# Two transformer blocks on one core: earlier table arithmetic, and five groups of transposes moved from TensorE to VectorE

## The chip, the core and the metric

The kernel runs on one core of one Trainium2 chip. Everything is float32. The metric is the device time of one launch in microseconds: the median of three runs is 2400.58 us (2400.37 to 2401.02).

## The reference

A sequence of 256 tokens, 2048 wide, goes through a gated delta-rule block with a Fourier branch and an MLP, and then through a second block with spatial gating, a state-space branch and cross attention. All weights together are 396 MB. Cut to what the change touches:

```python
# first block
qkv = silu(centred_short_conv(concat([q, k, v]), conv_w))       # 5 taps along the tokens, per channel
q = l2_norm(heads(q)) * DN_HEAD_DIM ** -0.5; k = l2_norm(heads(k)); v = heads(v)
x = x + (gate_a * y_a + gate_f * y_f) @ w_o[l]                   # y is "y_rows" before it is turned
# second block
dt = exp(log_dt); lam_bar = exp(lam * dt)                        # "tables" of the state-space branch
b_bar = ((lam_bar - 1) / lam)[:, :, None] * b_mat
k = (rms_norm_2(mem, mem_g) @ w_k).reshape(b, n_mem, XA_HEADS, XA_HEAD_DIM)   # "km"
v = (rms_norm_2(mem, mem_g) @ w_v).reshape(...)                               # "vm"
scores = einsum('bshd,bmhd->bhsm', qh, k) * XA_HEAD_DIM ** -0.5
merged = sum(gates * branch, axis=2); out = merged @ w_out
```

## The kernel before

The weights are cut into 396 units of 1 MB (128 partitions x 2048 numbers, four blocks of 128 rows by 512 columns). TensorE works through them in one fixed order. A product in float32 is made of three in TensorE's fast 32-bit format: the weight is split into `w_hi` and the rest `w_lo`, the activation likewise (`a_hi`, `a_lo` or `b_hi`, `b_lo` or `m_hi`, `m_lo`), and a unit is 24 matmuls of 128x512 (lines 2161, 2164, 2167): three products, four blocks, two halves of the 256 tokens.

Four engines share a unit n. SyncE issues the load of unit n into one of the buffers `raw` once TensorE is through with unit n - 4 (`weight`, L620 to L624, a wait on `pe_used`). ScalarE rounds it to `w_hi` (L794), VectorE forms `w_lo` in place of `raw` (L1253). Both do so two units ahead of TensorE: the split of unit n + 2 stands in slot n of their programs. TensorE waits on VectorE's `w_lo` (`lo_split`, L2143) at the start of a unit.

All other work is cut into steps, and `schedule()` gives each step a place, 2n (in the middle of unit n on TensorE, ahead of the split on the two other engines) or 2n + 1 (at the end of unit n, behind the split). Each engine runs its own part of a step at that place, in order; nothing is reordered at run time. A wait inside a step therefore holds up everything that stands behind it on that engine. This is true of SyncE too: a load of spilled rows that waits (`load_vm` for the attention's values, L699) has the next weights behind it.

The steps that the change touches:

- `conv_in`, `conv_silu`, `conv_norm`, `conv_root`: q and k of one half (512 columns, four heads) are turned to channels by tokens, by eight transposes on TensorE (L2272) which ScalarE copies into the padded tile `padT` (L955). VectorE applies the five taps (L1556, L1559), ScalarE the silu and the squares (L964, L970), TensorE sums the squares in 16 matmuls of one column (L2280). Half 0 of q and k lies at units 12 and 16, half 1 at units 48 and 52. v goes the same way and is not changed.
- `y_in(0)` and `merge_in(0)`: the first quarter (512 columns) of `y_rows`, the operand of `w_o` (units 88 to 103) and `w_out` (units 380 to 395). TensorE turns it in eight transposes (L2178), ScalarE writes `b_hi` (L808), VectorE `b_lo` (L1268).
- `ssm_small(0)` and `(1)`: the state-space branch's tables, 12 and 28 small VectorE operations on 128x32 numbers (L1734 to L1812) and a few on ScalarE, at slots 242 and 244.
- `xa_k`: the attention's keys `km_rows` are turned to `kmT` by 16 transposes on TensorE (L2398) and four copies on ScalarE (L1049) at the end of unit 333. The first to read them are the scores (`xa_score`, L2457) ahead of unit 338. `vm` is loaded over the place of `km_rows`, so `load_vm` waits until the keys are turned.

VectorE has its own transpose of 32x32 blocks: `turn_strips` (L1293) turns 512 columns of 256 rows in 16 instructions of 32 partitions x 256 numbers each.

Of the kernel before, what the change touches and what calls it, by code (L numbers as in the profile page):

```python
# [163 lines left out]
def schedule():  # L164
# [38 lines left out]
    for n in range(4):  # L203
# [4 lines left out]
        put_at(2 * end("w_dn_up", n) + 2, "y_in", n)  # L208
# [48 lines left out]
    put(end("xa_wv", 1) + 2, "ssm_small", 0)  # L257
    put(end("xa_wv", 1) + 4, "ssm_small", 1)
# [90 lines left out]
def build(nc, t_in, out, old, new):  # L349

    with ExitStack() as ctx:
# [432 lines left out]
        def _(act):  # L784
# [287 lines left out]
            def glu_rest():  # L1072
# [40 lines left out]
        def _(pool):  # L1113
# [1493 lines left out]
```

## Time and profile before

| | before |
|---|---|
| median of 3 runs | 2400.58 us (2400.37 to 2401.02) |
| the profiled execution's own time | 2403.19 us |
| its span in the trace | 2401.0 us |
| TensorE busy | 2379.5 us, 99% |
| VectorE busy | 1744.6 us, 73% |
| ScalarE busy | 1031.4 us, 43% |
| GpSimd busy | 272.6 us, 11% |
| share of the last chain: PE, DVE, DMA | 95%, 3%, 1% |
| moved by DMA | 475.16 MB, mean 198 GB/s |

The span is what the trace covers; the profiled execution took 2.19 us more than its span. Of the chain that ended last 95% is TensorE's own work, so nearly every microsecond of TensorE's work or idle time is one of the kernel's. The time of a wait has to be looked for at single units, since the shares are averages over 396 of them.

### The profile page before, as it was taken

What the parts mean: (1) busy time and instruction counts of PE and PEld (TensorE: products, weight loads), DVE (VectorE), ACT (ScalarE), POOL (GpSimd) and SP (SyncE); (2) the same over time, 40 slices, a digit from 0 to 9 for tenths busy, and PEclk for the clock granted to TensorE, in tenths of its full rate; (3) what the DMA queues carried; (4) which work ended last, traced back from release to release, by engine and by line L of the source; (5) the groups of instructions that cost most, each with busy time, mean ns of one, the idle gap of its engine ahead of it and who ended that gap; (6) DMA issues with size and microseconds to landing.
All of it is one profiled execution on the core that took longest, in us unless ns stands there. A gap on an engine that the chain in (4) does not pass through costs nothing.

```text
span 2401.0 us, 29968 instructions
## 1 busy us (share of the span) xinstructions
PE 2379.5 (99%) x12578; PEld 1950.2 (81%) x12578; DVE 1744.6 (73%) x1990; ACT 1031.4 (43%) x857; POOL 272.6 (11%) x226
## 2 busy tenths in 40 slices
PE   8999999999999999999999999999999999999998
PEld 7888788878888888888888888777777788888886
DVE  6465557557697887786766788989999967458865
ACT  5553345334344544444444435443334444544432
POOL 1002201210000000000000000055556400000000
PEclk9999999999999999999999999999999999999999
DMA  7343354347655555555555556565555586566753
GB/s 268 131 167 133 141 184 167 117 156 258 258 193 189 195 194 211 193 193 193 193 193 193 193 211 218 198 237 185 196 193 197 181 298 244 184 232 234 257 196 140
DMA packets 84230, 475.16 MB, mean 198 GB/s; under 512 B 8704, under 2 KB 8832, under 8 KB 32512
## 3 DMA queue, kind: packets, MB, share of 16 engines
q1 hardware_dynamic: 84096, 473.25, 55.5%
q8 instruction: 99, 1.62, 0.3%
q14 instruction: 35, 0.29, 0.0%
HBM read 450.15 MB, written 23.07 MB: 197 GB/s over the span
## 4 chain that ended last, share of the span: by engine, by line
PE 95%; DVE 3%; DMA 1%; issue 0%; ACT 0%; DVEq 0%; SPq 0%; ACTq 0%
PE acc L2161 29%; PE acc L2167 29%; PE acc L2164 29%; PE banks L2306 2%; PE banks L2355 1%; DVE w_lo L1253 1%; PE banks L2422 1%; PE banks L2435 1%; DMA raw<-in_w 1%; PE banks L2178 1%; DMA spilled<-stage 1%; PE banks L2475 0%; PE banks L2457 0%; PE banks L2280 0%; DMA gate_in<-spilled 0%
## 5 line engine op out<-in xcount | busy, mean ns | idle before, releaser
L1253 DVE TENSOR_TENSOR w_lo<-raw,w_hi 128x2048 fp32r<-128x2048 f32 x394 | 908.7, 2308 | 395.3 <-ACT w_hi L794 392.6
L794 ACT ACTIVATE w_hi<-raw 128x2048 fp32r<-128x2048 f32 x394 | 752.8, 1915 | 656.0 <-DMA raw<-in_w 655.8
L2161 PE MATMUL acc<-w_hi,a_hi 128*128 128x512 f32 x2112 | 838.2, 397 | 2.7 <-ACT a_hi L814 1.6
L2164 PE MATMUL acc<-w_lo,a_hi 128*128 128x512 f32 x2112 | 823.8, 390 | 0.0
L2167 PE MATMUL acc<-w_hi,a_lo 128*128 128x512 f32 x2112 | 823.7, 390 | 0.0
L2161 PEld LDWEIGHTS acc<-w_hi,a_hi 128*128 128x128 f32 x2112 | 397.0, 188 | 100.4 <-issue 15.4
L2167 PEld LDWEIGHTS acc<-w_hi,a_lo 128*128 128x128 f32 x2112 | 396.8, 188 | 84.7 <-DVE a_lo L1289 0.3
L2164 PEld LDWEIGHTS acc<-w_lo,a_hi 128*128 128x128 f32 x2112 | 397.4, 188 | 79.1
L2161 PE MATMUL acc<-w_hi,b_hi 128*128 128x512 f32 x928 | 361.7, 390 | 0.0
L2167 PE MATMUL acc<-w_hi,b_lo 128*128 128x512 f32 x928 | 361.1, 389 | 0.0
L2164 PE MATMUL acc<-w_lo,b_hi 128*128 128x512 f32 x928 | 361.0, 389 | 0.0
L2167 PEld LDWEIGHTS acc<-w_hi,b_lo 128*128 128x128 f32 x928 | 174.2, 188 | 36.1
L2164 PEld LDWEIGHTS acc<-w_lo,b_hi 128*128 128x128 f32 x928 | 174.2, 188 | 36.1
L2161 PEld LDWEIGHTS acc<-w_hi,b_hi 128*128 128x128 f32 x928 | 174.2, 188 | 36.0
L1300 DVE STREAM_TRANSPOSE b_raw<-hidden 32x256 f32<-32x256 f32 x256 | 111.5, 436 | 7.5
L1234 POOL MEMSET c_out<- 128x2048 f32 x1 | 1.8, 1817 | 1006.7 <-DMA spilled<-stage_b 1006.7
L893 ACT ACTIVATE stage<-acc,stats 128x512 f32<-128x512 f32 x72 | 45.6, 686 | 130.2 <-PE acc L2167 130.2
L1483 DVE TENSOR_TENSOR x_rows<-x_rows,acc 128x512 f32<-128x512 f32 x72 | 46.2, 683 | 31.1 <-PE acc L2167 31.0
L1204 POOL TENSOR_TENSOR rot<-pow_a,pow_b 128x256 f32<-128x256 f32 x32 | 47.6, 1488 | 176.8 <-DVE s_out L1918 130.4
L1904 DVE TENSOR_TENSOR_SCAN prod<-rad,prod 128x256 f32<-128x256 f32 x64 | 57.4, 956 | 0.6
L2161 PE MATMUL acc<-w_hi,m_hi 128*128 128x512 f32 x128 | 51.4, 401 | 2.2 <-DVE w_lo L1253 2.2
L1300 DVE STREAM_TRANSPOSE a_raw<-x_rows 32x256 f32<-32x256 f32 x112 | 48.8, 436 | 3.3
(353 smaller groups left out, 1681.3 us busy)
## 6 DMA issues: line engine op xcount, KB each, us to landing
raw<-in_w SPq DMA_DIRECT2D x395, 1024.0 KB, 4.8
spilled<-stage SPq DMA_DIRECT2D x72, 256.0 KB, 5.9
gate_in<-spilled SPq DMA_DIRECT2D x20, 512.0 KB, 5.8
x_rows<-in_x SPq DMA_DIRECT2D x4, 512.0 KB, 8.4
x_rows<-in_x SPq DMA_DIRECT2D x1, 2048.0 KB, 9.4
mem_rows<-in_mem SPq DMA_DIRECT2D x2, 1024.0 KB, 5.8
spilled<-stage_b SPq DMA_DIRECT2D x8, 256.0 KB, 5.9
out<-y_rows SPq DMA_DIRECT2D x3, 512.0 KB, 2.7
```

The source lines that it names most:

```text
L794: act.activation(w_hi[:, n % HIGH, :], raw[:, n % RAW, :], ACT.Copy)\
L893: act.activation(dst, src, func, scale=rms(norm, t)).then_inc(act_emptied, 1)
L1204: pool.tensor_tensor(c_[:, g], pa[0][:, g], pb[0][:, g], ALU.mult).then_inc(pool_done, me.done())
L1253: dve.tensor_tensor(w_lo[:, n % RAW, :], raw[:, n % RAW, :], w_hi[:, n % HIGH, :].bitcast(F32), ALU.subtract).then_inc(lo_split, 1)
L1300: dve.transpose(dst, src).then_inc(dve_done, me.done(*done_as))
L1483: ins = dve.tensor_tensor(x_rows[:, t, cs], x_rows[:, t, cs], src, ALU.add)
L1904: dve.tensor_tensor_scan(pr[z + 1][:, g], r_, pr[z][:, g], 0.0, ALU.mult, ALU.add)\
L2161: pe.matmul(o, hi[:, tk], wh, start=first, stop=False)
L2164: pe.matmul(o, hi[:, tk], wl, start=False, stop=False)
L2167: ins = pe.matmul(o, lo[:, tk], wh, start=False, stop=last)
L2178: ins = pe.transpose(b[:, q * P:(q + 1) * P], src(q), ident)
L2306: ins = pe.matmul(b[rs, cs], lhs[rs, cs], rhs(k, rs), start=True, stop=True)
```

## The change

Four kinds of work are moved. (1) `ssm_small(0)` and `(1)` run at slots 234 and 237 instead of 242 and 244. (2) q and k are turned by VectorE, straight from `qkv` into `padT`, by a new step `conv_turn`; the steps behind it (`conv_in`, `conv_silu`, `conv_norm`, `conv_root`) are given places three to five later. (3) The first quarters of y and of merge are turned by VectorE (`turn_first`, `first_hi`, `first_lo`). (4) The keys are turned by VectorE (`turn_plain("km", ...)`), and `load_vm` and the scores wait for VectorE.

```diff
     for half in (0, 1):
         for x, name in enumerate(("w_q", "w_k")):
             at = 2 * end(name, half) + 1
-            put_at(at, "conv_in", half, x, 0)
-            put_at(at + 2, "conv_in", half, x, 1)
-            put_at(at + 4, "conv_silu", half, x)
-            put_at(at + 6, "conv_norm", half, x)
+            for part in range(4):
+                put_at(at + part, "conv_turn", half, x, part)
+            put_at(at + 4, "conv_in", half, x, 0)
+            put_at(at + 5, "conv_in", half, x, 1)
+            put_at(at + 7, "conv_silu", half, x)
+            put_at(at + 9, "conv_norm", half, x)
             if x:
-                put_at(at + 8, "conv_root", half)
+                put_at(at + 11, "conv_root", half)
...
-        put_at(2 * end("w_dn_up", n) + 2, "y_in", n)
+        if n:
+            put_at(2 * end("w_dn_up", n) + 2, "y_in", n)
...
-        put_at(2 * end("w_branch1", n) + 2, "merge_in", n)
+        if n:
+            put_at(2 * end("w_branch1", n) + 2, "merge_in", n)
     f = end("w_dn_up", 3)
     put(f + 1, "load_mem", 0)
+    for tag, name in (("y", "w_dn_up"), ("merge", "w_branch1")):
+        at = 2 * end(name, 0) + 2
+        for part in range(6):
+            put_at(at + part, "turn_first", tag, part)
+        put_at(at + 6, "first_hi", tag)
+        put_at(at + 8, "first_lo", tag)
...
-    put(end("xa_wv", 1) + 2, "ssm_small", 0)
-    put(end("xa_wv", 1) + 4, "ssm_small", 1)
+    put(end("xa_wv", 0) - 2, "ssm_small", 0)
+    put(end("xa_wv", 0) + 1, "ssm_small", 1)
...
     for part in range(8):
         put_at(2 * a + 17 + part, "turn_plain", "sg", part)
+        put_at(2 * a + 25 + part, "turn_plain", "km", part)
     put_at(2 * a + 26, "plain_hi", "sg")
     put_at(2 * a + 28, "plain_lo", "sg")
     put(a + 10, "gelu_turn")
     a = max(a + 13, end("w2_xg", 1) + 1)
     put(a - 1, "load_xq")
-    put(a, "xa_k")
     put(a + 1, "load_vm")
...
             def load_mem(t):
                 if t == 0:
                     sp.wait_ge(pe_done, me.at("y.T"))
...
             def load_vm():
-                sp.wait_ge(pe_done, me.at("km.T"))
+                sp.wait_ge(dve_done, me.at("km.T"))
                 load_rows(vm, "xa_wv", loaded["vm"])
...
+            def first_hi(tag):
+                act.wait_ge(dve_done, me.at(f"{tag}.first.T"))
+                for t in range(NT):
+                    at = (slice(None), slice(0, 4), slice(t * P, (t + 1) * P))
+                    act.activation(b_hi[0][at], b_raw[0][at], ACT.Copy).then_inc(act_done, me.done(f"{tag}.{t}.hi"))
...
+            def conv_turn(half, x, part):
+                if part == 0:
+                    dve.wait_ge(act_emptied, emptied(INDEX[(("w_q", "w_k")[x], half)], "act"))
+                    dve.wait_ge(pool_done, me.at("pad1" if half else "pad0"))
+                    if x == 0 and half:
+                        dve.wait_ge(pe_done, me.at("scan0.3.out.PE"))
+                    if x:
+                        dve.wait_ge(dve_done, me.at(f"conv{half}0.sum"))
+                rows = padT[:, :, 2:2 + T]
+                turn_strips(qkv[:, x], rows, 4 * part, 4, (f"conv{half}{x}.turned",))
+
             def conv_in(half, x, part):
-                dve.wait_ge(act_done, me.at(f"conv{half}{x}.pad0", f"conv{half}{x}.pad1"))
+                if x < 2:
...
+            def turn_first(tag, part):
+                name = {"y": "w_fourier", "merge": "w_branch0"}[tag]
+                if part == 0:
+                    dve.wait_ge(pe_used, end(name, 3))
+                    dve.wait_ge(dve_done, me.at("w_dn_up0.y" if tag == "y" else "w_branch10.y"))
+                turn_strips(y_rows[:, :, 0:NW], b_raw[0][:, 0:4, :], 3 * part, min(3, 16 - 3 * part), (f"{tag}.first.T",))
+
+            def first_lo(tag):
+                for t in range(NT):
+                    at = (slice(None), slice(0, 4), slice(t * P, (t + 1) * P))
+                    dve.wait_ge(act_done, me.at(f"{tag}.{t}.hi"))
+                    dve.tensor_tensor(b_lo[0][at], b_raw[0][at], b_hi[0][at].bitcast(F32), ALU.subtract)\
+                        .then_inc(dve_done, me.done(f"{tag}.{t}.lo"))
...
             def turn_plain(tag, part):
                 raw_rows = PLAIN[tag][0]
                 if part == 0:
                     if tag == "xo":
                         dve.wait_ge(pe_used, end("w2_gate2", 3))
-                    dve.wait_ge(dve_done, me.at({"sg": "sg.gated", "xo": "xo.rows", "glu": "glu.rows"}[tag]))
+                    if tag == "km":
+                        dve.wait_ge(loaded["km"], 32)
+                        dve.wait_ge(dve_done, me.at("sg.T"))
+                    else:
+                        dve.wait_ge(dve_done, me.at({"sg": "sg.gated", "xo": "xo.rows", "glu": "glu.rows"}[tag]))
```

Before, VectorE's program in half 1 of the convolution reads, from the six splits that end with unit 46's on (`w_lo`; `convT<-padT` are the taps, `nrm` the norms):

```order
L1253 TENSOR_TENSOR w_lo<-raw,w_hi 128x2048 x6
L1556 TENSOR_SCALAR convT<-padT,small 128x256 x2
L1559 SCALAR_TENSOR_TENSOR convT<-padT,small,convT 128x256 x8
L1253 TENSOR_TENSOR w_lo<-raw,w_hi 128x2048
L1556 TENSOR_SCALAR convT<-padT,small 128x256 x2
L1559 SCALAR_TENSOR_TENSOR convT<-padT,small,convT 128x256 x8
L1253 TENSOR_TENSOR w_lo<-raw,w_hi 128x2048 x2
L1568 TENSOR_SCALAR nrm<-banks 128x2x4
L1576 RECIPROCAL nrm<-nrm 128x2x4
L1253 TENSOR_TENSOR w_lo<-raw,w_hi 128x2048
```

Now the turns (`padT<-qkv`, eight instructions for half of the 512 columns) stand ahead of the splits, and the two sets of taps come together:

```order
L1271 TENSOR_TENSOR w_lo<-raw,w_hi 128x2048 x6
L1318 STREAM_TRANSPOSE padT<-qkv 32x2x4x32 x8
L1271 TENSOR_TENSOR w_lo<-raw,w_hi 128x2048
L1318 STREAM_TRANSPOSE padT<-qkv 32x2x4x32 x8
L1271 TENSOR_TENSOR w_lo<-raw,w_hi 128x2048
L1588 TENSOR_SCALAR convT<-padT,small 128x256 x2
L1591 SCALAR_TENSOR_TENSOR convT<-padT,small,convT 128x256 x8
L1588 TENSOR_SCALAR convT<-padT,small 128x256 x2
L1591 SCALAR_TENSOR_TENSOR convT<-padT,small,convT 128x256 x8
L1271 TENSOR_TENSOR w_lo<-raw,w_hi 128x2048 x2
L1318 STREAM_TRANSPOSE padT<-qkv 32x2x4x32 x4
L1600 TENSOR_SCALAR nrm<-banks 128x2x4
```

Between the splits of units 46 and 47 there was one set of taps and there are now eight turns; both sets of taps stand behind unit 48's split. The first sum of squares (`nrm<-banks`) moves behind the turns of k.

At the state-space tables VectorE's program read, ahead of the splits of units 238, 239 and 240 (`a_raw<-x_rows` are turns of the next block's input, `a_lo` its low part):

```order
L1300 STREAM_TRANSPOSE a_raw<-x_rows 32x2x4x32 x2
L1322 TENSOR_TENSOR a_raw<-a_raw,stats 128x4x128 x2
L1300 STREAM_TRANSPOSE a_raw<-x_rows 32x2x4x32 x2
L1253 TENSOR_TENSOR w_lo<-raw,w_hi 128x2048
L1300 STREAM_TRANSPOSE a_raw<-x_rows 32x2x4x32 x4
L1253 TENSOR_TENSOR w_lo<-raw,w_hi 128x2048
L1329 TENSOR_TENSOR a_lo<-a_raw,a_hi 128x4x128 x2
L1300 STREAM_TRANSPOSE a_raw<-x_rows 32x2x4x32 x4
L1253 TENSOR_TENSOR w_lo<-raw,w_hi 128x2048
```

Now the 28 operations of `ssm_small(1)` (`ssm_t`) follow the split of unit 239, the first six of them shown, and unit 240's split comes behind all of them:

```order
L1271 TENSOR_TENSOR w_lo<-raw,w_hi 128x2048
L1318 STREAM_TRANSPOSE a_raw<-x_rows 32x2x4x32 x4
L1271 TENSOR_TENSOR w_lo<-raw,w_hi 128x2048
L1347 TENSOR_TENSOR a_lo<-a_raw,a_hi 128x4x128 x2
L1318 STREAM_TRANSPOSE a_raw<-x_rows 32x2x4x32 x2
L1788 TENSOR_TENSOR ssm_t<-ssm_t 128x32
L1790 TENSOR_SCALAR ssm_t<-ssm_t 128x32
L1792 TENSOR_SCALAR ssm_t<-ssm_t 128x32
L1794 TENSOR_SCALAR ssm_t<-ssm_t 128x32
L1796 TENSOR_TENSOR ssm_t<-ssm_t 128x32
L1798 TENSOR_TENSOR ssm_t<-ssm_t 128x32
```

The 12 operations of `ssm_small(0)` stand in the same way between the splits of units 236 and 237. Both groups came behind the split of unit 243 before.

At the attention's keys VectorE's program had, from the split of unit 333 on (`b_raw<-av` are turns of the spatial gate, `b_lo<-b_raw` their low part):

```order
L1253 TENSOR_TENSOR w_lo<-raw,w_hi 128x2048
L2013 STREAM_TRANSPOSE b_raw<-av 32x2x8x32 x4
L1253 TENSOR_TENSOR w_lo<-raw,w_hi 128x2048 x2
L2020 TENSOR_TENSOR b_lo<-b_raw,b_hi 128x4x128 x4
L1253 TENSOR_TENSOR w_lo<-raw,w_hi 128x2048 x4
L1979 TENSOR_REDUCE stats<-banks 128x2
```

Now it has four groups of turned keys (`kmT<-km_rows`, 16 instructions in all) between the splits of units 334 to 338:

```order
L1271 TENSOR_TENSOR w_lo<-raw,w_hi 128x2048
L2063 STREAM_TRANSPOSE b_raw<-av 32x2x8x32 x4
L1271 TENSOR_TENSOR w_lo<-raw,w_hi 128x2048
L2063 STREAM_TRANSPOSE kmT<-km_rows 32x2x8x32 x4
L1271 TENSOR_TENSOR w_lo<-raw,w_hi 128x2048
L2063 STREAM_TRANSPOSE kmT<-km_rows 32x2x8x32 x4
L2070 TENSOR_TENSOR b_lo<-b_raw,b_hi 128x4x128 x4
L1271 TENSOR_TENSOR w_lo<-raw,w_hi 128x2048
L2063 STREAM_TRANSPOSE kmT<-km_rows 32x2x8x32 x4
L1271 TENSOR_TENSOR w_lo<-raw,w_hi 128x2048
L2063 STREAM_TRANSPOSE kmT<-km_rows 32x2x8x32 x4
L1271 TENSOR_TENSOR w_lo<-raw,w_hi 128x2048 x2
```

The last turned keys stand behind the split of unit 337 in VectorE's program. On SyncE the order does not move, but the semaphore that `vm` waits for does. Before:

```order
L624 DMA raw<-in_w 128x2048 [waits pe_used] x2
L634 DMA vm<-spilled 128x2x512 [waits spill_stored1,spill_stored0,pe_done]
L634 DMA vm<-spilled 128x2x512 [waits spill_stored3,spill_stored2]
L624 DMA raw<-in_w 128x2048 [waits pe_used] x2
L741 DMA spilled<-stage 128x512 [waits act_emptied] x2
L624 DMA raw<-in_w 128x2048 [waits pe_used] x4
```

Now (the two weights behind `vm` are units 338 and 339):

```order
L635 DMA raw<-in_w 128x2048 [waits pe_used] x2
L645 DMA vm<-spilled 128x2x512 [waits spill_stored1,spill_stored0,dve_done]
L645 DMA vm<-spilled 128x2x512 [waits spill_stored3,spill_stored2]
L635 DMA raw<-in_w 128x2048 [waits pe_used] x2
L753 DMA spilled<-stage 128x512 [waits act_emptied] x2
L635 DMA raw<-in_w 128x2048 [waits pe_used] x4
```

`pe_done` has become `dve_done` in the row of `vm`, and the rows behind it are the same.

## Rows read from the trace of the kernel before

**Rows 1.** The page, busy time of each engine and weight issues to landing.

```profile
PE 2379.5 (99%) x12578; PEld 1950.2 (81%) x12578; DVE 1744.6 (73%) x1990; ACT 1031.4 (43%) x857; POOL 272.6 (11%) x226
...
raw<-in_w SPq DMA_DIRECT2D x395, 1024.0 KB, 4.8
```

**Rows 2.** Chain of waits: start, duration, what, xcount.

```profile
121.99 1.68 PE banks L2280 x16
...
361.36 0.87 PE banks L2272 x8
...
2027.61 1.75 PE banks L2398 x16
```

**Rows 3.** Timeline of PE: start, duration, instruction, idle time before it.

```profile
1462.99 0.39 PE L2161 MATMUL acc<-w_hi,m_hi 128*128 128x512 f32 x1
...
1501.80 0.40 PE L2167 MATMUL acc<-w_hi,m_lo 128*128 128x512 f32 x1
...
1504.36 0.80 PE L2161 MATMUL acc<-w_hi,m_hi 128*128 128x512 f32 x1 [2.17 <-DVE w_lo L1253]
...
1511.57 0.39 PE L2161 MATMUL acc<-w_hi,a_hi 128*128 128x512 f32 x1
...
1527.66 0.39 PE L2167 MATMUL acc<-w_hi,a_lo 128*128 128x512 f32 x1
...
1529.17 0.47 PE L2161 MATMUL acc<-w_hi,a_hi 128*128 128x512 f32 x1 [1.12 <-DVE pow_b L1845]
```

**Rows 4.** Windows, all engines; PEclk is the granted clock, 1.00 full.

```profile
1500.00:1520.00 20.00, 17.83 (x72) 14.23 (x71) 17.57 (x29) 8.28 (x7) 0.77 (x1) 0.91 0.54 188
```

**Rows 5.** Timeline of DVE between 1436 and 1505.

```profile
1436.04 2.29 DVE L1253 TENSOR_TENSOR w_lo<-raw,w_hi 128x2048 fp32r<-128x2048 f32 x1 [1.14 <-ACT w_hi L794]
...
1455.22 2.29 DVE L1253 TENSOR_TENSOR w_lo<-raw,w_hi 128x2048 fp32r<-128x2048 f32 x1
...
1466.29 2.29 DVE L1253 TENSOR_TENSOR w_lo<-raw,w_hi 128x2048 fp32r<-128x2048 f32 x1 [1.50 <-ACT w_hi L794]
...
1481.12 0.18 DVE L1734 TENSOR_SCALAR ssm_t<-small 128x32 f32<-128x32 f32 x1
...
1495.53 0.20 DVE L1756 TENSOR_TENSOR ssm_t<-ssm_t 128x32 f32<-128x32 f32 x1
...
1502.02 2.28 DVE L1253 TENSOR_TENSOR w_lo<-raw,w_hi 128x2048 fp32r<-128x2048 f32 x1
```

**Rows 6.** Timeline of DVE around the convolution and two other places.

```profile
334.62 2.29 DVE L1253 TENSOR_TENSOR w_lo<-raw,w_hi 128x2048 fp32r<-128x2048 f32 x1 [4.92 <-ACT w_hi L794]
...
387.42 0.61 DVE L1556 TENSOR_SCALAR convT<-padT,small 128x256 f32<-128x256 f32 x2 [2.33 <-ACT padT L955]
...
394.81 2.28 DVE L1253 TENSOR_TENSOR w_lo<-raw,w_hi 128x2048 fp32r<-128x2048 f32 x1
...
1398.00 1.83 DVE L1300 STREAM_TRANSPOSE a_raw<-x_rows 32x256 f32<-32x256 f32 x4
...
619.07 1.29 DVE L1268 TENSOR_TENSOR b_lo<-banks,b_hi 128x512 fp32r<-128x512 f32 x2 [2.52 <-ACT b_hi L808]
```

**Rows 7.** Timeline of ACT between 372 and 374.

```profile
372.68 1.06 ACT L964 ACTIVATE kT<-convT 128x1024 f32<-128x1024 f32 x1 [4.10 <-DVE convT L1559]
```

**Rows 8.** Timeline of PE at units 53 and 88.

```profile
386.45 0.48 PE L2161 MATMUL acc<-w_hi,a_hi 128*128 128x512 f32 x1
...
633.20 0.39 PE L2161 MATMUL acc<-w_hi,b_hi 128*128 128x512 f32 x1
```

**Rows 9.** Timeline of DVE where the attention's keys are due.

```profile
2018.99 2.92 DVE L2013 STREAM_TRANSPOSE b_raw<-av 32x512 f32<-32x512 f32 x4
```

**Rows 10.** Timeline of SP: two weight issues behind a load of rows.

```profile
2175.21 4.86 SPq L624 DMA_DIRECT2D raw<-in_w  x2
```

**Rows 11.** Timeline of ACT: the split that waited for the first.

```profile
2182.51 1.92 ACT L794 ACTIVATE w_hi<-raw 128x2048 fp32r<-128x2048 f32 x1 [8.67 <-DMA raw<-in_w]
```

**Rows 12.** Timeline of PE at unit 338.

```profile
2054.30 0.58 PE L2161 MATMUL acc<-w_hi,a_hi 128*128 128x512 f32 x1
```

More of the change, by code:

```diff
@@ L574, in build @@
                  "xo": (a_raw[:, 0:KW, :], a_hi[:, 0:KW, :], a_lo[:, 0:KW, :]),
+                 "km": (kmT[:, :, :],),
                  "glu": (a_raw[:, KW:, :], a_hi[:, KW:, :], a_lo[:, KW:, :])}
@@ L665, in load_mem @@
                     sp.wait_ge(pe_done, me.at("y.T"))
+                    sp.wait_ge(dve_done, me.at("y.first.T"))
                 else:
@@ L949, in conv_in @@
             def conv_in(half, x, part):
+                if x < 2:
+                    return
                 for b in range(2 if part == 0 else 0):
@@ L1043, in turned @@
             def turned(tag, dst, scale):
-                if tag == "km":
-                    act.wait_ge(dve_done, me.at("sg.T"))
                 for j in range(4):
@@ L1090, in _ @@
                      "sg_norm": lambda part: root("sgn", 64, NT) if part == 0 else None,
-                     "gelu_turn": gelu_turn, "plain_hi": plain_hi,
-                     "xa_k": lambda: turned("km", kmT, 1.0), "xa_q": lambda: turned("xq", xqT, 1.0 / 16),
+                     "gelu_turn": gelu_turn, "plain_hi": plain_hi, "first_hi": first_hi,
+                     "xa_q": lambda: turned("xq", xqT, 1.0 / 16),
                      "xa_score": xa_score, "xa_prob": xa_prob, "xa_out": xa_out,
@@ L1234, in ssm_small @@
                 pool.memset(c_out[:, :, :, :], 0.0).then_inc(pool_done, me.done("c_out.zero"))
-            steps = {"conv_in": lambda half, x, part: pads(half) if (x, part) == (0, 0) else None,
+            steps = {"conv_turn": lambda half, x, part: pads(half) if (x, part) == (0, 0) else None,
                      "key_rows": key_rows, "gram": gram, "decay": decay, "turn": turn, "solve_x": solve_x, "fold": fold,
@@ L1539, in fourier @@
                         .then_inc(dve_done, me.done(f"fourier{g}.lo"))
+            def conv_turn(half, x, part):
[8 more added lines that the diff above has]
+                turn_strips(qkv[:, x], rows, 4 * part, 4, (f"conv{half}{x}.turned",))
             def conv_in(half, x, part):
-                dve.wait_ge(act_done, me.at(f"conv{half}{x}.pad0", f"conv{half}{x}.pad1"))
+                if x < 2:
+                    dve.wait_ge(dve_done, me.at(f"conv{half}{x}.turned"))
+                else:
+                    dve.wait_ge(act_done, me.at(f"conv{half}{x}.pad0", f"conv{half}{x}.pad1"))
                 dve.wait_ge(pool_done, me.at("pad1" if half else "pad0"))
@@ L2042, in tables @@
                     .then_inc(dve_done, me.done("w_sc.lo"))
-            steps = {"tables": tables, "scalars": scalars, "fourier": fourier, "conv_in": conv_in,
+            steps = {"tables": tables, "scalars": scalars, "fourier": fourier, "conv_turn": conv_turn, "conv_in": conv_in,
                      "conv_norm": conv_norm, "conv_root": conv_root, "key_rows": key_rows, "decay": decay, "turn": turn, "solve_x": solve_x,
@@ L2059, in _ @@
                      "ssm_small": ssm_small, "ssm": ssm, "sg_norm": sg_norm, "sg_mix": sg_mix,
-                     "gelu_turn": gelu_turn, "xa_score": xa_score, "turn_plain": turn_plain, "plain_lo": plain_lo,
+                     "gelu_turn": gelu_turn, "xa_score": xa_score, "turn_plain": turn_plain, "turn_first": turn_first, "first_lo": first_lo, "plain_lo": plain_lo,
                      "xa_gate": xa_gate, "glu_rest": glu_rest, "glu_gate": glu_gate}
@@ L2263, in conv_in @@
             def conv_in(half, x, part):
-                if part:
+                if part or x < 2:
                     return
@@ L2452, in xa_score @@
             def xa_score(h):
-                pe.wait_ge(act_done, me.at("km.3.t", "xq.3.t"))
+                pe.wait_ge(dve_done, me.at("km.T"))
+                pe.wait_ge(act_done, me.at("xq.3.t"))
                 b = take_bank("xs", h, f"xa{h}.exp")
@@ L2485, in glu_rest @@
                     ins.then_inc(pe_done, me.done(f"gr.{j}.T", "gelu_rows.T"))
-            def xa_k():
-                pe.wait_ge(loaded["km"], 32)
-                turned("km", lambda t, k: km_rows[:, t, k * P:(k + 1) * P])
             def xa_q():
@@ L2500, in _ @@
                      "ssm_u": ssm_u, "ssm": ssm, "sg_mix": sg_mix,
-                     "xa_k": xa_k, "xa_q": xa_q, "xa_score": xa_score, "xa_prob": xa_prob,
+                     "xa_q": xa_q, "xa_score": xa_score, "xa_prob": xa_prob,
                      "xa_out": xa_out, "glu_rest": glu_rest,
```

3 lines of the change are left out of this document (2 added, 1 removed).

## The prediction

> **What bounds the kernel now.** I read the page first: TensorE is busy for 99% of the span [rows 1]. The chain of waits comes next: its small pieces are the transposes and column sums that stand between units, 0.87 us for eight transposes, 1.75 for sixteen, 1.68 for sixteen column sums [rows 2]. They are on the path, and so is what they become if VectorE is late: the timeline of PE shows the two places near the tables where it waited (2.17 and 1.12 us) [rows 3]. So each part is a balance: TensorE work removed, against how late VectorE's split `w_lo` comes at the next units. For the second I rebuild VectorE's queue from its timeline in the new order and compare it with the start of the unit on PE.
>
> **Removed from TensorE.** Eight transposes go at each of four places of the convolution (3.48 us) and at the two first quarters (1.74), sixteen at the keys (1.75) [rows 2]. Total 6.97 us. The column sums only move one and a half units later.
>
> **Tables.** Before, unit 247 started 2.56 us after the last matmul of unit 246, where 0.23 is usual: 2.33 lost. It then took 7.21 us (1504.36 to 1511.57) [rows 3]. Usual is 5.58: from 1462.99 to 1501.80 are seven units less one matmul, 167 steps of 0.2324, and 24 of these. The difference, 1.63, is the clock: PE was granted 0.91 of full speed in the window from 1500 to 1520, which means that it ran at 1.2 GHz for part of it, after the 2.17 us without work [rows 4, 3]. The second wait cost 1.51 − 0.23 = 1.28 [rows 3], and the clock did not fall after it. Together 5.24 us come back if the operations no longer hold anything up there. I count on all of it, because 9 us less stand ahead of units 247 to 251 on VectorE; if only the second wait stays, 1.28 less comes back.
>
> In their new place 28 operations (1495.53 to 1502.02, 6.49 us, 0.232 each) and 12 more (2.7 at the same step) stand ahead of the split of unit 240 [rows 5]. That split began at 1455.22, with no idle time before it; the next idle time of VectorE in the row behind is 1.50 at 1466.29. So all 9.2 us push it: it starts at 1464.4 and ends 2.3 later, at 1466.7. PE wants it at 1462.99 [rows 3]. A wait of 3.7 us is new. It is longer than the 2.17 after which the clock fell, so I add the same 1.63. This part is then −5.24 + 3.7 + 1.63 = +0.1, or −1.5 if the clock stays up. ScalarE's share costs nothing: its table loads lie beside VectorE's queue, which is the later one; were that cover gone they would add to the same wait. From 1466.29 on VectorE has idle time to catch up, and unit 241 follows in time.
>
> **Convolution.** Turning 512 columns takes 16 instructions. Four of the same shape took 1.83, so eight take 3.7 and sixteen 7.4 [rows 6]. Two sets of taps take 394.81 − 387.42 = 7.4 [rows 6]. In half 1 VectorE starts the split of unit 46 at 334.62 [rows 6]. In the new order: +2.3 split, +3.7 turns, +2.3 split (unit 47), +3.7 turns, +2.2 split (48), +7.4 taps, so q's taps end at 356.3. Then the silu, 1.06, squares of the same size, and the split of 1.92 on ScalarE follow [rows 7, 11], 4.1 in all, and the split of unit 50 can start at 360.4. Behind it: 2.3 + 1.9 + 0.4 (norm) + 1.9 + 2.3 + 3.7 + 2.2 + 7.4 = 22.1, and the split of unit 53 ends at 384.85. PE wants it at 386.45 [rows 8] less two groups of transposes (1.74) and less the 1.70 of column sums that now come behind unit 53: 383.0. New wait 1.8. The same reckoning gives 0.1 at unit 49, and in half 0 0.25 at unit 21 and 0.5 at unit 23. Together 2.65 against 3.48 removed: −0.8. Its bounds: −3.5 if VectorE is never late, and +0.8 plus 1.6 if the clock falls at unit 53.
>
> **First quarters.** The turns wait for `y_rows`, and VectorE's queue sets the end. The second quarter's `b_lo` starts at 619.07 [rows 6] and ends at 620.3; three turns (1.4), unit 87's split (2.3), two products and a sum of the gates (2.5), and the last turn follow: 626.9. ScalarE's `first_hi` ends at 627.9 and its split at 629.8, VectorE's split of unit 88 at 632.1, a pair `b_lo` and the pair `first_lo` (pairs like these took 1.29 [rows 6], started 1.25 apart) at 634.6. PE wants the operand at 633.20 [rows 8]. The transposes taken away here lay at unit 83, ahead of all of this, so both sides come 0.87 earlier and the difference stays. New wait 1.4. Merge has the same steps in the same order. Two times 1.4 against 1.74 removed: +1.06. Bounds: −1.74 if the operand is in time, +2.9 with 2.3 each.
>
> **Keys.** VectorE turns them in 16 instructions, four in 2.92 [rows 9]. After the four at 2018.99 its queue has no gap in the new order: unit 334's split (2021.93 to 2024.26), then 2.94 turns, 2.33 split, 2.94, 2.45 low part, 2.33, 2.94, 2.33, 2.94: the keys are turned at 2045.5. TensorE had done so by 2029.4 [rows 2]. The scores come later and do not wait. But the load of `vm` waits for the keys on SyncE, and behind it stand the weights of units 338 and 339, as the two rows of the change show. They are issued at 2046.5, some 12 us later than before. What a weight takes then: the row of the page says 4.8 us, with nothing ahead of it [rows 1]. Two weights issued at 2175.21 right behind a 1 MB load of rows, as here, let ScalarE start at 2182.51, 7.3 later [rows 10, 11]. I take 7.3, the case that is like this one: split on ScalarE from 2053.8 to 2055.75, on VectorE until 2058.05. PE wants unit 338 at 2054.30 [rows 12] − 1.75 = 2052.55. New wait 5.5 us, 3.0 with a landing in 4.8, and 1.63 for the clock, as after 2.17 us. Net: −1.75 counted above, +7.1 here.
>
> The Trainium skill ("DMA: Bandwidth & Descriptors", Queues, rings and completion order) says that the descriptors of an issuing engine's row are consumed in ring order on each DMA engine. By that rule the weight's data start behind those of `vm`, which speaks for 7.3 and not 4.8; the rows at 2175 agree.
>
> **Sum.** −6.97 −5.24 + (3.7 + 1.63) + 2.65 + 2.8 + (5.5 + 1.63) = +5.7 us. The profiled execution took 2403.19 and would take 2408.9; the median lies 2.6 lower, so I predict 2400.58 + 5.7 = **2406.3 us**. What a measurement here can tell from no change I take as 0.2%, 4.8 us.
>
> **Rivals.**
> - *Cheaper waits.* The weights behind `vm` land in 4.8 us (−2.5) and the clock stays up after both long waits (−3.3): 2400.5. For it: the 4.8 of the page is the median of 395 [rows 1], and the clock did not fall after 1.12 us [rows 3]. Against it: it fell after 2.17, and both new waits are longer than that.
> - *The change does what it looks like and VectorE is never late* (the other side). All that is removed comes back, 6.97 + 5.24 = 12.2: 2388.4. It needs VectorE's idle time, 27% of the span, to lie at these places. It decides at unit 240 and at unit 338: below 5.5 us of pushed work ahead of unit 240's split, and with the keys turned before 2040, no wait arises. Against it: VectorE's rows have no gap where the 9.2 us and the 11.8 us of key turns are put.
> - *The clock falls at the shorter waits too.* Units 53, 88 and 380 wait for 1.4 to 1.8 us, between the 1.12 that did not lower the clock and the 2.17 that did [rows 3]. At 1.63 each, 4.9 more: 2411.2, and with the operands another 0.85 late at both quarters 2412.9. Against it: 1.12 did nothing.
> - *Transposes count as rest.* Eight transposes of v end right ahead of unit 53's wait, so that TensorE does no large matmul for 0.87 + 1.8 = 2.7 us there, more than the 2.17 that lowered the clock [rows 2, 3]. Then the clock falls there alone: 2406.3 + 1.6 = 2407.9.
>
> The Trainium skill ("TensorE: Matmul & The Clock Gate", Part 4: PE-mode transpose) says that transposes do not count as TensorE being busy. That is the mechanism of the last rival; the trace shows eight transposes at 0.109 us each [rows 2] and no wait behind such a group, so it decides nothing.
>
> **How the numbers follow.** Forecast 0.48, its own range 2403.5 to 2409.5, from landing and clock each going one way. The bound of 4.8 us lies at 2405.4, inside it, so two thirds of it are slower (0.32) and a third is within (0.16). Cheaper waits 0.20, within. The change does what it looks like 0.09, faster. Lower clock at short waits 0.13 and transposes as rest 0.06, slower. Remaining 0.04: small mistakes in the queues that cancel, within. Faster 0.09, same 0.40, slower 0.51. The range from 2400 to 2411.5 leaves out the 0.09 and the upper part of the rival with the lower clock, and holds the bounds of landing and clock.
>
> **What the new profile would show.** PE: no wait left at unit 247, one of about 3.7 at unit 240 released by `w_lo`, one of 3 to 5.5 at unit 338 with a granted clock under 1.00 in the window behind each. SP: `vm` issued at about 2045 in the old times, with two weights right behind. Waits of 1 to 2 us at units 53, 88 and 380. The prediction is wrong if unit 338 starts without a wait, which would mean that the keys were turned by 2040 or that the weights do not stand behind `vm`, or if unit 240 waits for less than 1 us.

## The result and the profile after

The changed kernel takes 2412.35 us (2410.87 to 2413.80, 5 runs) against 2400.58 before (2400.32 to 2401.52, 5 runs): a ratio of 1.0045, 95% interval 1.0033 to 1.0056. It is slower, by more than the 4.8 us that can be told from no change. The forecast was 2406.3, with a range up to 2411.5: the direction was right, the amount about half of what came, and the median lies 0.85 above the range. In a second set of runs the same kernel took 2411.56 (2410.10 to 2412.68) beside 2401.44 before, where one of the 21 runs of before took 3411.25 us and leaves the median where it is.

The profiled execution took 2411.5, with a span of 2409.7, 8.7 more than before's. The page, where TensorE has 64 matmul instructions less and 5.3 us less work than in [rows 1]:

```profile
PE 2374.2 (99%) x12514; PEld 1942.2 (81%) x12514; DVE 1799.2 (75%) x2102; ACT 1025.9 (43%) x845; POOL 267.9 (11%) x226
```

The timeline of PE shows what came in their place. The columns are those of [rows 3]; these are all the places after the first 60 us where TensorE waited for more than 1 us:

```profile
383.88 0.50 PE L2211 MATMUL acc<-w_hi,a_hi 128*128 128x512 f32 x1 [1.44 <-DVE w_lo L1271]
```

```profile
633.04 0.47 PE L2211 MATMUL acc<-w_hi,b_hi 128*128 128x512 f32 x1 [1.48 <-issue]
```

```profile
1462.70 0.40 PE L2217 MATMUL acc<-w_hi,m_lo 128*128 128x512 f32 x1
...
1466.99 0.77 PE L2211 MATMUL acc<-w_hi,m_hi 128*128 128x512 f32 x1 [3.89 <-DVE w_lo L1271]
...
1467.55 0.63 PE L2214 MATMUL acc<-w_lo,m_hi 128*128 128x512 f32 x1
...
1474.04 0.40 PE L2211 MATMUL acc<-w_hi,m_hi 128*128 128x512 f32 x1
```

```profile
1531.10 0.47 PE L2211 MATMUL acc<-w_hi,a_hi 128*128 128x512 f32 x1 [1.55 <-DVE pow_b L1877]
```

```profile
2060.68 0.79 PE L2211 MATMUL acc<-w_hi,a_hi 128*128 128x512 f32 x1 [5.08 <-DVE w_lo L1271]
...
2061.28 0.63 PE L2214 MATMUL acc<-w_lo,a_hi 128*128 128x512 f32 x1
...
2068.17 0.47 PE L2211 MATMUL acc<-w_hi,a_hi 128*128 128x512 f32 x1
```

```profile
2310.47 0.47 PE L2211 MATMUL acc<-w_hi,b_hi 128*128 128x512 f32 x1 [1.48 <-issue]
```

In order of time these are units 53 (1.44 us idle), 88 (1.48), 240 (3.89), 251 (1.55), 338 (5.08) and 380 (1.48). Unit 247, which had waited 2.17 [rows 3], is gone from the list; unit 251 is still on it, but not for the same reason (see the experiments). The second matmul of units 240 and 338 takes 0.63 instead of 0.39, which is the lower clock of 1.2 GHz, and the granted clock of these stretches is 0.91, as it was behind unit 247 before [rows 4]. Behind the four waits of 1.4 to 1.6 us no matmul is slow. At units 88 and 380 the profile names no releaser ("issue"). VectorE's own timeline has it: the low part of the first quarter (`first_lo`, L2040) ends at 632.93, 0.11 before unit 88 starts.

```profile
631.65 1.28 DVE L2040 TENSOR_TENSOR b_lo<-b_raw,b_hi 128x512 fp32r<-128x512 f32 x2
```

The windows:

```profile
1460.00:1480.00 20.00, 16.11 (x64) 12.71 (x63) 18.93 (x36) 6.90 (x7) 0.00 (x0) 0.91 0.49 165
...
2050.00:2070.00 20.00, 14.92 (x62) 11.95 (x61) 7.83 (x7) 9.48 (x10) 0.00 (x0) 0.91 0.79 290
```

How VectorE got late at unit 240, in its own timeline (unit 239's split, the turn ahead of the 28 operations, the turn behind them, unit 240's split; [rows 5] had that split at 1455.22):

```profile
1452.49 2.29 DVE L1271 TENSOR_TENSOR w_lo<-raw,w_hi 128x2048 fp32r<-128x2048 f32 x1
...
1456.02 0.90 DVE L1318 STREAM_TRANSPOSE a_raw<-x_rows 32x256 f32<-32x256 f32 x2
...
1463.61 0.90 DVE L1318 STREAM_TRANSPOSE a_raw<-x_rows 32x256 f32<-32x256 f32 x2
...
1464.55 2.29 DVE L1271 TENSOR_TENSOR w_lo<-raw,w_hi 128x2048 fp32r<-128x2048 f32 x1
```

Nothing is idle between them, and the split ends at 1466.84, 0.15 before TensorE starts.

And at the keys. VectorE's last turn, SyncE's load of `vm` with the two weights behind it, and ScalarE's first split of these:

```profile
2045.33 2.92 DVE L2063 STREAM_TRANSPOSE kmT<-km_rows 32x512 f32<-32x512 f32 x4
```

```profile
2048.28 0.89 SPq L645 DMA_DIRECT2D vm<-spilled  x2
...
2049.22 0.93 SPq L635 DMA_DIRECT2D raw<-in_w  x2
```

```profile
2056.40 1.91 ACT L806 ACTIVATE w_hi<-raw 128x2048 fp32r<-128x2048 f32 x1 [11.92 <-DMA raw<-in_w]
```

From the issue of the weights at 2049.22 to the split are 7.2 us, about the 7.3 behind the 1 MB load at 2175 [rows 10, 11], and ScalarE had been idle for 11.92 us.

### The profile page after: what moved, and what is told of

Same layout as the page of the kernel before. It is cut to its first block, busy times and chain, and to the rows that moved or that the text cites. A ratio compares the mean times of both kernels' runs of the same rounds, so it can differ in the third digit from the quotient of the medians.

```text
span 2409.7 us, 29932 instructions
## 1 busy us (share of the span) xinstructions
PE 2374.2 (99%) x12514; PEld 1942.2 (81%) x12514; DVE 1799.2 (75%) x2102; ACT 1025.9 (43%) x845; POOL 267.9 (11%) x226
## 4 chain that ended last, share of the span: by engine, by line
PE 87%; DVE 8%; DMA 2%; issue 1%; ACT 1%; SPq 0%; DVEq 0%; ACTq 0%
PE acc L2211 27%; PE acc L2214 26%; PE acc L2217 26%; DVE w_lo L1271 2%; PE banks L2356 2%; DMA raw<-in_w 2%; PE banks L2405 1%; DVE convT L1591 1%; DVE padT L1318 1%; ACT w_hi L806 1%; PE banks L2472 1%; PE banks L2485 1%; DVE a_raw L1318 1%; DVE kmT L2063 0%; PE banks L2228 0%
## 5 line engine op out<-in xcount | busy, mean ns | idle before, releaser
L2211 PE MATMUL acc<-w_hi,a_hi 128*128 128x512 f32 x2112 | 838.7, 397 | 11.8 <-DVE w_lo L1271 8.4
```

Of the source, the lines that this page charges most:

```text
L2211: pe.matmul(o, hi[:, tk], wh, start=first, stop=False)
```

## The experiments

All times of one table line were taken beside the kernel before on the same chip. The first set (the four kernels with one part undone) had 18 runs of before (median 2401.58), the second (changed again, vm later, tables at 240) 21 (2401.44), the third (the last three) 27 (2401.89). The changed kernel was not run in the first set, so what a part is worth when undone is a difference between two sets. The changed kernel lay 11.8 us above before beside the result and 10.1 in the second set: differences of one or two microseconds are therefore read from the traces, and the medians only say whether they agree.

| kernel | median us (lowest to highest), runs | ratio to before, 95% |
|---|---|---|
| changed, again | 2411.56 (2410.10 to 2412.68), 5 | 1.0042 [1.0030, 1.0055] |
| changed, keys on TensorE | 2406.95 (2404.39 to 2408.22), 11 | 1.0022 [1.0013, 1.0030] |
| changed, tables at the old slots | 2407.99 (2406.74 to 2408.95), 8 | 1.0026 [1.0016, 1.0036] |
| changed, first quarters on TensorE | 2409.95 (2408.32 to 2410.22), 5 | 1.0033 [1.0021, 1.0046] |
| changed, convolution on TensorE | 2410.08 (2409.65 to 2413.69), 5 | 1.0035 [1.0022, 1.0049] |
| changed, vm loaded later | 2405.21 (2403.05 to 2407.62), 11 | 1.0016 [1.0007, 1.0026] |
| changed, tables at 240, c_in earlier | 2406.83 (2402.94 to 2408.95), 11 | 1.0022 [1.0013, 1.0031] |
| all mended | 2396.81 (2394.92 to 2397.66), 11 | 0.9978 [0.9969, 0.9987] |
| before with the mended tables alone | 2397.36 (2397.00 to 2399.57), 11 | 0.9985 [0.9976, 0.9994] |
| all mended, convolution on TensorE | 2396.44 (2395.00 to 2397.64), 11 | 0.9978 [0.9970, 0.9987] |

To read the traces beside each other I take TensorE's starts of units as marks and the time from one mark to the next. It is free of the first 60 us: the start of unit 8, at 57 to 58.5 us, varied by 1.5 us among the thirteen traces. The times, in us:

| stretch (from unit to unit) | before, twice | changed, twice | what it holds |
|---|---|---|---|
| 10 to 14 | 32.53, 32.49 | 30.01, 30.01 | transposes of q, half 0 |
| 15 to 60 | 327.63, 327.64 | 328.09, 328.19 | rest of the convolution |
| 82 to 92 | 58.00, 58.00 | 58.84, 58.85 | first quarter of y |
| 235 to 251 | 94.06, 92.86 | 96.06, 96.31 | tables |
| 333 to 342 | 58.69, 58.69 | 63.78, 63.45 | keys |
| 374 to 384 | 58.00, 58.00 | 58.87, 58.86 | first quarter of merge |

**Undoing one part at a time.** The four kernels are the changed one with one part of the diff taken back.

Keys on TensorE:

```diff
-        put_at(2 * a + 25 + part, "turn_plain", "km", part)
+    put(a, "xa_k")
...
-                sp.wait_ge(dve_done, me.at("km.T"))
+                sp.wait_ge(pe_done, me.at("km.T"))
```

> The changed kernel with one part undone: the keys are turned by TensorE again and vm waits for TensorE. Theory (the load of vm holds up two weights, unit 338 waits 5.2 us and the clock falls behind it): the waits of 5.2 and 1.5 us go and 1.75 us of transposes come back, 5.0 us faster than the changed kernel, 2407.4; no step longer than 0.3 us is left between units 334 and 340. Rival (the keys on VectorE are a gain and the loss is made elsewhere): 1.75 us slower, 2414.1.

It came out 4.6 us below the changed kernel (2406.95 against 2411.56), against 5.0 expected, and the stretch from 333 to 342 is 58.70 again, as before the change. The rival is out.

Tables at the old slots:

```diff
-    put(end("xa_wv", 0) - 2, "ssm_small", 0)
-    put(end("xa_wv", 0) + 1, "ssm_small", 1)
+    put(end("xa_wv", 1) + 2, "ssm_small", 0)
+    put(end("xa_wv", 1) + 4, "ssm_small", 1)
```

> The changed kernel with the table operations at their old slots 242 and 244. Theory (in their new place they make a wait of 4.1 at unit 240 and a slow unit 240 of 1.5, in the old one 2.3 and 1.6 at unit 247, and the wait at unit 251 has another cause but is 0.4 shorter): 2.0 us faster, 2410.3. Rival of the prediction (both old waits come back, 5.24, against 5.3): no difference, 2412.3.

3.6 us below the changed kernel, more than the 2.0. Neither sentence had it: unit 247 waited again, but for 1.11 us and not for 2.17, and the clock stayed at 1.00. The stretch from 235 to 251 took 92.40, which is 3.7 and 3.9 less than in the two traces of the changed kernel.

```profile
1502.54 0.50 PE L2211 MATMUL acc<-w_hi,m_hi 128*128 128x512 f32 x1 [1.11 <-DVE w_lo L1271]
```

```profile
1500.00:1520.00 20.00, 18.73 (x81) 14.76 (x80) 17.71 (x24) 8.29 (x7) 1.82 (x1) 1.00 0.60 211
```

First quarters on TensorE (`y_in` and `merge_in` at n = 0 again, `turn_first`, `first_hi` and `first_lo` not scheduled):

```diff
-        if n:
-            put_at(2 * end("w_dn_up", n) + 2, "y_in", n)
+        put_at(2 * end("w_dn_up", n) + 2, "y_in", n)
```

> The changed kernel with both first quarters turned by TensorE again. Theory (a wait of 1.65 at units 88 and 380 against 0.9 of transposes each): 1.5 us faster, 2410.8. Rival (in most runs the clock falls at both waits too, though not in the profiled one): 1.5 + 3.3 = 4.8 us faster, 2407.6, and a higher mean granted clock than the changed kernel has. Other rival (VectorE hides it): 1.7 slower, 2414.1.

1.6 us below the changed kernel. That alone would be within the spread of the sets; the traces show it, since both stretches are 58.00 again, 0.84 and 0.87 less. No slow matmul stood behind units 88 and 380 in the seven traces that wait there, so the rival with the lower clock is not borne out.

Convolution on TensorE (`conv_turn` not scheduled, `conv_in`, `conv_silu`, `conv_norm`, `conv_root` at their old places, the copies into `padT` on ScalarE again):

```diff
-            for part in range(4):
-                put_at(at + part, "conv_turn", half, x, part)
-            put_at(at + 4, "conv_in", half, x, 0)
+            put_at(at, "conv_in", half, x, 0)
```

> The changed kernel with q and k of the convolution turned by TensorE again. Theory (3.5 us of transposes against waits of 0.6, 0.5, 0.1 and 1.5 us at units 21, 23, 49 and 53, all at full clock): 0.9 us slower, 2413.2. Rival (the clock falls behind the wait of unit 53 in most runs): 0.7 us faster, 2411.6. Where the clock falls near 100 us for the transposes of q, 1.6 slower again, as in the profiled run of before: 2414.8.

The median is 1.5 us below the changed kernel, where 0.9 above was expected, on 5 runs that spread over 4.0. By the marks the part is worth -0.4 to the changed kernel: from 10 to 14 30.86 here against 30.01, and from 15 to 60 327.6 against 328.1. What varies is the clock near 100 us. Before's two traces lost 1.65 there (32.5 against 30.86), this one nothing:

```profile
90.00:110.00 20.00, 20.00 (x122) 17.70 (x122) 11.22 (x21) 10.73 (x15) 0.00 (x0) 1.00 0.40 138
```

while the kernel with the quarters undone, which has no transposes of q at all there, lost 1.6:

```profile
90.00:110.00 20.00, 20.00 (x107) 17.50 (x106) 11.01 (x18) 8.70 (x10) 0.00 (x0) 0.91 0.38 145
```

So the low clock there does not belong to the transposes. In before's first trace it shows ahead of them too: the four matmuls of 128x130 that end the stretch of small ones took 1.07 us at 98.66 and 0.61 at 88.85. The clock fell in 3 of 8 traces with q on VectorE and in 3 of 5 with q on TensorE.

**The kernel before, in a second trace**, since undoing the tables had given a wait of another length.

> The kernel before once more, one look. Theory (the wait of 2.3 at unit 247 hangs on when unit 244's weight lands, and the profile of before caught a late one): here that weight is split on ScalarE up to 1.8 us earlier against unit 244, the wait is 1.3, and the clock does not fall behind it: about 2400.5, 2.6 below the profiled time. Rival (the wait and the fall are fixed costs, and before's profile is slow for another reason): the wait of 2.3 and the slow unit 247 are there again.

It took 2401.56, and the wait at unit 247 was 1.56 us and not 2.17. The clock did not fall. The next wait, at unit 251, was longer than in [rows 3]:

```profile
1503.51 0.51 PE L2161 MATMUL acc<-w_hi,m_hi 128*128 128x512 f32 x1 [1.56 <-DVE w_lo L1253]
...
1527.72 0.47 PE L2161 MATMUL acc<-w_hi,a_hi 128*128 128x512 f32 x1 [1.65 <-DVE pow_b L1845]
```

```profile
1500.00:1520.00 20.00, 18.29 (x79) 14.44 (x78) 17.60 (x27) 8.28 (x7) 1.81 (x1) 1.00 0.64 217
```

The cause of the difference stands 27 us ahead of the wait's end. Unit 244's split on VectorE waited for ScalarE 0.83 us here; in before's profile it waited longer and started 0.85 later, and there is no idle time on VectorE between it and unit 247. Of the 0.85, 0.25 is TensorE's own shift (1501.55 against 1501.80), and 0.6 is the difference of the waits:

```profile
1476.94 2.29 DVE L1253 TENSOR_TENSOR w_lo<-raw,w_hi 128x2048 fp32r<-128x2048 f32 x1 [0.83 <-ACT w_hi L794]
```

```profile
1477.79 2.29 DVE L1253 TENSOR_TENSOR w_lo<-raw,w_hi 128x2048 fp32r<-128x2048 f32 x1 [1.27 <-ACT w_hi L794]
```

ScalarE in turn had waited for the weight (4.27 here, 4.72 there). It was issued at 1468.51 here and at 1468.75 there, and ScalarE started 6.5 and 7.1 us later. Of the 2.33 us in the first profile some 0.6 were thus a later weight's. The slow clock came with them, in this one trace only; that the length of the wait brought it is the likely reading, but no run tests it. The theory named the right place and missed the size (1.7 and not 1.3).

**The changed kernel again.**

> The changed kernel once more, beside the runs that the next ones are compared with. If the single steps of the traces are all there is, its profile shows the same waits (1.5 at unit 53, 1.65 at 88 and 380, 4.1 at 240, 1.7 at 251, 5.2 at 338) and the slow clock behind 240 and 338 alone. If the 3 us by which its median stands above the step count come from the clock, its slow stretches are longer than 1.5 us each or more in number.

The same six waits stood there, with slow matmuls behind units 240 and 338 alone. But in the other kernels of this study the slow clock did not always cost 1.5 us. In six traces the start of unit 241 came 7.05, 7.22, 8.20, 7.23, 8.32 and 8.45 us after that of unit 240 (5.57 at full clock), and in six that of 339 came 7.49, 7.58, 7.54, 8.63, 8.38 and 8.31 after 338 (6.03). Means: 2.2 and 2.0 lost, and not 1.63. The long one, from the trace of the kernel with `vm` later, in which the granted clock of the window was lower:

```profile
1460.00:1480.00 20.00, 16.11 (x58) 12.59 (x57) 19.12 (x32) 6.78 (x7) 0.00 (x0) 0.83 0.38 140
```

**The load of vm behind the two weights.** The keys stay on VectorE.

```diff
-    put(a + 1, "load_vm")
+    put(a + 3, "load_vm")
```

> The changed kernel with the load of vm two slots later, behind the weights of units 338 and 339; the keys stay on VectorE. Theory (it is the load's place in SyncE's queue that costs): the wait at unit 338 and the slow unit behind it go, 6.9 us faster than the changed kernel, 2405.5, and 1.7 faster than with the keys on TensorE. Rival (VectorE's 11.8 us of key turns make units 334 to 340 late by themselves): a wait of over 1 us stays at one of these units.

6.35 us below the changed kernel (2405.21 against 2411.56). The stretch from 333 to 342 takes 56.89, which is 1.8 less than before, and unit 338 starts without a wait. SyncE's timeline has the four weights ahead of the load:

```profile
2025.22 16.65 SPq L635 DMA_DIRECT2D raw<-in_w  x4
...
2048.34 0.88 SPq L645 DMA_DIRECT2D vm<-spilled  x2
...
2049.28 5.26 SPq L635 DMA_DIRECT2D raw<-in_w  x2
```

VectorE turned the keys as late as in the changed kernel (`vm` was issued at 2048.34 and at 2048.28), so its queue was never what held unit 338. Unit 338's weight, issued at 2036.10 with nothing but weights ahead of it, landed 4.75 us later. The rival is out: what cost the time is the load's place in SyncE's queue.

**The tables at slot 240, c_in earlier.**

```diff
-    put(end("xa_wv", 0) + 1, "ssm_small", 1)
+    put(end("xa_wv", 1), "ssm_small", 1)
...
-    put(end("xa_wk", 1) - 1, "load_c")
+    put(end("xa_wk", 1) - 3, "load_c")
```

> The changed kernel with the 28 table operations behind the split of unit 242 instead of 239 (slot 240), and the load of c_in two slots earlier. Theory: VectorE has 3.9 us of idle time at units 242 to 244, so of the wait of 4.1 at unit 240 and of its slow unit at most 0.3 stays (at unit 243); the wait of 1.7 at unit 251 goes, since it stands behind 2.8 us of waiting for c_in: 6.8 us faster, 2405.6. Rival (the wait at 251 has VectorE's c_eff work as its cause): 1.2 to 1.7 us stay at unit 251, 2407.

4.7 us below the changed kernel and not 6.8. A wait came up at unit 243 and one stayed at 251:

```profile
1481.10 0.50 PE L2211 MATMUL acc<-w_hi,m_hi 128*128 128x512 f32 x1 [0.86 <-DVE w_lo L1271]
...
1526.64 0.47 PE L2211 MATMUL acc<-w_hi,a_hi 128*128 128x512 f32 x1 [1.07 <-DVE pow_b L1877]
```

The 1.03 at unit 243 (0.86 idle and the slower start) is the slack that I had read from before, used up by 28 operations.

Unit 251 needs more. Ahead of its split VectorE has 5.5 us of C products (`c_eff` to `c_out`), which need both unit 250's split and the landing of `c_in`. In the changed kernel it was `c_in` that came last:

```profile
1523.12 0.69 DVE L1853 TENSOR_TENSOR c_eff<-c_in,ssm_t 128x512 f32<-128x512 f32 x1 [2.84 <-DMA c_in<-in_c_im]
```

The kernel with the first quarters undone has the same tables, but there `c_in` came earlier, and unit 251 waited 0.12 us only:

```profile
1521.59 0.69 DVE L1844 TENSOR_TENSOR c_eff<-c_in,ssm_t 128x512 f32<-128x512 f32 x1 [1.42 <-DMA c_in<-in_c_im]
```

In all six traces with the tables at 234 and 237 VectorE's wait for `c_in` (2.98, 2.84, 2.75, 2.67, 1.73 and 1.42 us) is 1.3 us more than TensorE's at unit 251 (1.68, 1.55, 1.42, 1.37, 0.42 and 0.12). So VectorE's own work left 1.3 us of slack there, and the landing of `c_in` made the wait. With the tables at their old slots it was different: `c_in` was in time, and unit 250's split was late. In before's first trace VectorE started it 1.1 us after TensorE had started unit 249, in the second 2.2 and with the tables put back 2.2, where it is 0.6 us ahead of that start in the changed kernel. ScalarE, which rounds the weight first, had been held up by VectorE's `stats`:

```profile
1516.05 0.20 ACT L859 ACTIVATE stats<-stats 128x2 f32<-128x2 f32 x1 [1.72 <-DVE stats L1387]
```

In this run, with the tables at 240, the split came 0.5 us after unit 249's start, and the copy ahead of the products (`rad`) took 1.30 us instead of 0.17. Together they use up the slack and leave the 1.07 us. The rival had the size right. That the C products alone make the wait it did not show, and why the copy took longer stays open; it ended at the same time as GpSimd's `memset` of `c_out` (1518.5).

**All mended.** The tables one slot later still, and the C products behind unit 251's split.

```diff
-    put(end("xa_wv", 0) + 1, "ssm_small", 1)
+    put(end("xa_wv", 1) + 1, "ssm_small", 1)
...
-        put_at(2 * end("xa_wk", 1) - 2 + 2 * part, "ssm_small", part)
+        put_at(2 * end("xa_wk", 1) - 2 + 2 * part + (part == 2), "ssm_small", part)
...
-    put(end("xa_wk", 1) - 1, "load_c")
-    put(a + 1, "load_vm")
+    put(end("xa_wk", 1) - 3, "load_c")
+    put(a + 3, "load_vm")
```

> All mended: the load of vm two slots later, the 28 table operations at slot 241, the C products (ssm_small 2) behind unit 251's split instead of ahead of it, c_in loaded two slots earlier, both first quarters on TensorE; q, k and the keys stay on VectorE. Theory, against the kernel before: units 235 to 252 in 89.3 us instead of 93.1 (-3.8), keys -1.8, convolution -0.4, together -6.0: 2395.4, with waits of over 1 us at unit 53 alone, and a granted clock that falls nowhere behind unit 60. Rival (the steps that are moved again make others late, as slot 240 did with 1.0 at unit 243): 1 to 3 us stay at units 243 to 252, 2397 to 2398.

2396.81: 5.1 us faster than before in the same set, and 14.7 below the changed kernel of the set before it. One wait is left at the tables, 0.78 us at unit 244, somewhat less than the rival's 1 to 3. The profile puts it down to ScalarE, but VectorE's split of unit 244, behind the 28 operations, ends at 1484.07, 0.15 us ahead of TensorE's start, as at unit 240 above:

```profile
1484.22 0.47 PE L2202 MATMUL acc<-w_hi,m_hi 128*128 128x512 f32 x1 [0.78 <-ACT stage_b L896]
```

The stretch from 235 to 251, which is the one that the expectation priced (it names 252), takes 89.83 (93.46 before, mean of two; 89.3 expected), and 333 to 342 takes 56.89.

**The tables alone, on the kernel before.**

> The kernel before with the table part alone, mended as in the version with all: operations at slots 234 and 241, the C products behind unit 251's split, c_in two slots earlier. Theory: -3.8 against the kernel before, 2397.6, nothing else moves. Rival (as above): -1 to -2.5.

2397.36 against 2401.89 is -4.5 by the medians, -3.8 by the means (2397.72 against 2401.48). The stretch from 235 to 251 takes 89.83, 3.6 less than the mean of before's two. The rival is out.

**All mended, convolution on TensorE.**

> As the version with all mended, but q and k of the convolution on TensorE. Theory (the traces: 0.86 less between units 10 and 14, 0.46 more from 15 to 60 with VectorE turning): 0.4 us slower than with VectorE turning, 2395.8. Rival (the runs: undoing this part took 0.7 us off the changed kernel): 0.7 us faster, 2394.7.

2396.44 and 2396.81 with intervals that are almost the same: no difference can be measured between turning q and k on VectorE and on TensorE. Neither expectation is borne out; both were smaller than the spread.

## Why the prediction was half right

- *Keys*: +5.4 net predicted, +5.1 and +4.8 in the two traces, -4.6 when undone. The queue on VectorE, the blocked load and the landing of 7.3 us (7.2) all came as worked out [rows 9 to 12]. The rival with cheap waits is out.
- *First quarters*: +1.06 predicted, +1.7 in the traces, -1.6 when undone. The wait cost 1.65 each and not 1.4.
- *Convolution*: -0.8 predicted, -0.4 by the marks. The runs do not show it: undone in the changed kernel it gave -1.5, in the mended one -0.4, both within what the medians vary. Waits of 0.5 (unit 21), 0.5 (23), 0.04 (49) and 1.5 (53) against the 0.25, 0.5, 0.1 and 1.8 that I had.
- *Tables*: +0.1 predicted, +3.2 and +3.5 in the traces against before's second one, -3.6 when undone. This is the step that failed: "I count on all of it", the 5.24 us that should come back. It was wrong in two of its terms, and the price of the clock in a third.
  - Unit 247. The wait of 2.17 and the slow clock behind it [rows 3, 4] stood in before's one profile, but not in its second trace, nor with the tables back in the changed kernel: 1.1 to 1.6 us idle and a full clock there. From the start of unit 241 to that of 249 the changed kernel took 44.5 and 44.7. Against the first profile (48.45) the 3.96 did come back, as reckoned; against the other two (46.72 and 46.31) only 1.6 to 2.2 did.
  - Unit 251. The 1.28 did not come back. The old wait went with the tables, and one for the landing of `c_in`, which had been hidden behind it, took its place. The prediction did not ask what else the C products wait for.
  - Unit 240. The wait cost 4.06 and not 3.7, and the slow clock behind it 2.2 on average, where I had 1.63 from the one instance.

  So some 1.6 to 2.2 came back and not 5.24, and 4.06 + 2.2 was paid and not 5.3. (The two traces show 3.2 and 3.5 in all, as their falls were of the shorter kind.) The profile itself had the warning, a profiled execution 2.6 us above the median: I carried the difference over to the forecast as if it were spread evenly.
- *The clock at short waits*: I gave chances of 0.13 and 0.06 to a fall behind waits of 1.4 to 1.8. None of these waits, in any trace, had slow matmuls behind it, also where eight transposes ended right ahead of it at unit 53. The Trainium skill ("TensorE: Matmul & The Clock Gate", Part 4: PE-mode transpose) says that a transpose does not count as TensorE being busy in the same way; at 0.87 + 1.44 us none of eight traces shows a consequence of it.
- *Sum*: the three parts undone are worth 4.6 + 3.6 + 1.6 = 9.8, the convolution something between -0.4 and 1.5, and the second set measured 10.1 between the two kernels (2411.56 - 2401.44), the set of the result 11.8. Nothing of the size of another part is left over, but a microsecond or two could be.

What stays open is when the clock falls near 100 us, between the small matmuls of the gates and the transforms: it did so in 6 of 13 traces, with q turned on either engine, and costs 1.6 us.

## What to carry to other kernels

Before pricing a wait that a change removes, ask whether the profiled execution is the median's: if it is slower by more than one term of the sum, one of its waits is an accident of that execution, and the largest is the first to suspect. When a wait goes, ask what ended just before it: at unit 251 one wait made room for another of the same length. When a buffer's release moves to another engine, look at what stands behind the load that waits for it in the issuing queue; moving the load two slots later was worth more (6.4 us) than the transposes that had been saved (1.75). Work moved ahead of a deadline has to fit the slack of every unit that it passes, not just clear the place where it was in the way.

## What the runs showed of the hardware

The clock's fall has a price that varies with the execution: behind one and the same wait of 4.06 us at unit 240, TensorE lost between 1.5 and 2.9 us at 1.2 GHz (granted clock of the window 0.91 or 0.83). After the kernel's opening (in every trace the first matmuls are slow, until 10 to 13 us) some forty idle times of 0.8 to 1.7 us were never followed by it; the one of 2.17 and all of 3.89 and more were. A 1 MB weight issued right behind a 1 MB load of rows reached ScalarE 7.2 us after its issue; the same weight with the load moved away landed after 4.75, and the median of 395 weights is 4.8 [rows 1].
